# Nine more slabs of an encoder kernel's input projection as seven products of quarters, on one core

## What is computed

```
xa (1024)  ya (1024)  u, v (1024 each)  z (1024)  xbc (2048)  dt (16)  gates gA, gB, gC (1024 each)
branch A: xa -> conv over 4 tokens -> two small products (lg) -> linear recurrence, times gelu(ya)
branch B: gelu(u) * (layernorm(gelu(v)) mixed within blocks of 128 tokens)
branch C: silu(conv(xbc)) -> x, B, C of a chunked state-space scan; times silu(z); normalised
x += W_out(sum of sigmoid(gate) * projection of each branch)
x += cross attention over 256 memory tokens;  x += top-2 of 32 experts (width 512);  out = rmsnorm(x)
```

## Time and profile before

| what | value |
|---|---|
| median of 3 runs | 996.18 us |
| lowest and highest run | 995.7 and 999.54 us |
| span of the profiled execution, first to last instruction | 992.8 us |
| PE busy | 848.5 us, 85% of the span |
| PEld busy | 641.3 us, 65% |
| DVE busy | 293.7 us, 30% |
| ACT busy | 192.6 us, 19% |
| POOL busy | 211.2 us, 21% |
| HBM read | 283.08 MB, 286 GB/s over the span |

### The profile page before, as it was taken

The page is one execution under the profiler, slowest core; times in us unless marked ns, Lnnn a source line. Parts: engine busy times, 40 slices in busy tenths (PEclk is TensorE's granted clock), DMA queues, the critical chain, the costliest instruction groups (busy, mean ns, idle before and its releaser), DMA issues.

```text
span 992.8 us, 17255 instructions
## 1 busy us (share of the span) xinstructions
PE 848.5 (85%) x7608; PEld 641.3 (65%) x7608; DVE 293.7 (30%) x785; ACT 192.6 (19%) x354; POOL 211.2 (21%) x120
## 2 busy tenths in 40 slices
PE   8999999999999999999999999666676666666575
PEld 8888866888999999999479555333333333333342
DVE  2344101646164433342111552121221221121212
ACT  2321126851022000101111221111101111101102
POOL 1000000003999878994001000000000000000000
PEclk9999999999999999999999999987987998988987
DMA  9734524342454444444994799999999999999995
GB/s 304 217 126 158 196 101 170 128 170 85 170 212 171 171 169 166 157 161 167 430 363 158 314 426 426 426 428 427 426 428 425 428 427 428 426 426 426 426 427 203
DMA packets 62399, 285.24 MB, mean 287 GB/s; under 512 B 6692, under 2 KB 11640, under 8 KB 50168
## 3 DMA queue, kind: packets, MB, share of 16 engines
q1 hardware_dynamic: 52736, 278.96, 70.2%
q10 hardware_dynamic: 9592, 5.19, 2.0%
HBM read 283.08 MB, written 1.06 MB: 286 GB/s over the span
## 4 chain that ended last, share of the span: by engine, by line
PE 62%; DMA 28%; SPq 4%; another core or an unknown queue 2%; DVE 1%; POOL 1%; issue 1%; ACT 0%; DVEq 0%; POOLq 0%
PE bank L1639 20%; PE bank L1468 20%; DMA ring<-in_w_gate_up_dram 15%; DMA ring<-in_w_down_dram 10%; PE bank L1480 6%; PE bank L1822 5%; SPq L398 4%; DMA blk<-in_w_gate_up_dram 3%; PE bank L1844 2%; PE bank L1541 1%; PE bank L1791 1%; PE bank L1715 1%; PE bank L1695 1%; PE bank L1600 0%
## 5 line engine op out<-in xcount | busy, mean ns | idle before, releaser
L1468 PE MATMUL bank<-blk,ring 128*128 128x256 f32 x896 | 198.5, 383 | 0.8 <-DVE blk L1237 0.8
L1468 PEld LDWEIGHTS bank<-blk,ring 128*128 128x128 f32 x896 | 170.3, 191 | 25.5 <-issue 1.4
L1639 PE MATMUL bank<-ring 128*128 128x128 f32 x1088 | 127.4, 275 | 0.4 <-POOL ring L507 0.4
L1639 PEld LDWEIGHTS bank<-ring 128*128 128x128 f32 x1088 | 124.3, 192 | 0.7 <-issue 0.6
L1822 PE MATMUL bank<-ring,cbm 128*32 128x256 f32 x1088 | 80.5, 446 | 48.5 <-DMA ring<-in_w_gate_up_dram 48.1
L1639 PE MATMUL bank<-blk,ring 128*128 128x128 f32 x816 | 96.7, 275 | 0.1
L1639 PEld LDWEIGHTS bank<-blk,ring 128*128 128x128 f32 x816 | 94.1, 192 | 0.9 <-issue 0.8
L1822 PEld LDWEIGHTS bank<-ring,cbm 128*32 128x32 f32 x1088 | 40.1, 125 | 81.3 <-issue 61.7
L480 POOL TENSOR_TENSOR ring<-ring 128x1024 f32<-128x1024 f32 x17 | 40.1, 2356 | 241.9 <-PE bank L1601 230.9
L1326 DVE TENSOR_TENSOR cbm<-bank,gq 128x256 f32<-128x256 f32 x32 | 13.6, 424 | 251.3 <-PE bank L1791 251.3
L1822 PE MATMUL bank<-blk,cbm 128*32 128x256 f32 x768 | 57.9, 452 | 31.9 <-DMA blk<-in_w_gate_up_dram 31.9
(11 more groups left out here) (307 smaller groups left out, 842.5 us busy)
## 6 DMA issues: line engine op xcount, KB each, us to landing
ring<-in_w_gate_up_dram SPq DMA_DIRECT2D x34, 2048.0 KB, 49.9
blk<-in_w_gate_up_dram SPq DMA_DIRECT2D x24, 2048.0 KB, 50.3
ring<-in_w_in_dram SPq DMA_DIRECT2D x19, 2048.0 KB, 7.7
ring<-in_w_down_dram SPq DMA_DIRECT2D x18, 2048.0 KB, 49.5
blk<-in_w_down_dram SPq DMA_DIRECT2D x10, 2048.0 KB, 49.5
params<-in_w_gate_up_dram SPq DMA_DIRECT2D x6, 2048.0 KB, 50.0
ring<-in_w_kv_dram SPq DMA_DIRECT2D x4, 2048.0 KB, 7.9
params<-in_w_down_dram SPq DMA_DIRECT2D x3, 2048.0 KB, 51.2
```

Source lines behind the costliest of these rows:

```text
L1468: last = mm(ps[:, f * T:(f + 1) * T], w[:, k, c:c + P], src[:, k, :], start=k == 0, stop=k == KD - 1)
L1639: last = mm(ps[:, f * P:(f + 1) * P], wt[:, k, f * P:(f + 1) * P], xt[:, k, :], start=k == 0, stop=k == 3)
```

## The change

- Nine slabs go from the dense to the seven-product form: xbc 1 to 3, xa 0 and 1, z 0 and 1, v 0 and 1. Slab 0 of xbc, u, ya and the first slab of gA stay dense. There are 26 seven-product slabs instead of 17.
- Input sums of hT for them are made once, into a new place TE (block 6); the weight sums and the copied and added middles of slabs ahead of pA 0 live in blocks 5 and 8 (`weight_sums`, `middles`).
- Quarters are kept interleaved in a bank (`part`), so that two neighbouring quarters form one run of 256 tokens for each column tile. This holds for all 26 slabs.
- For xbc and xa DVE adds the products inside the banks (`conv_sums`), and conv_init and the taps read them there. z and v are folded into their tiles, and ACT then applies silu and gelu in place to halves of 1024 elements (`silu_z`, `gelu_v`). For v the tokens stand in the array and 256 columns of weights stream (`in_rows`).
- The eight lg units come four behind each v slab instead of two behind each v unit. DVE's exponents(0) and (1) move ahead of the fold of v, and its product on L983 behind it. The softplus part of ACT moves from the third conv_init to behind the small loads, and silu of two units is done behind each slab's `mids`.
- The banks of a seven-product slab are taken one at a time as its products come to them, not all four ahead of the first.
- PE waits for `read["xn"]` ahead of the q slabs.

The core of the diff (the new helpers, and where they are used):

```diff
+    for h in range(1, 4):
+        order += seven("xbc", h)
+    order += seven("xa", 0) + seven("xa", 1) + ["cs0"]
+    order += seven("z", 0) + [f"xs{i}" for i in range(4)] + seven("z", 1) + [f"cb{i}" for i in range(GROUPS)]
+    for h in range(2):
+        order += seven("v", h) + [f"lg{j}" for j in range(4 * h, 4 * h + 4)]
...
+        TA, TB, TE = (block(b).rearrange("p (q k t) -> p q k t", q=4, t=P) for b in (10, 9, 6))
+        EARLY = SEVEN["pA", 0]
+        def weight_sums(j):
+            two, one = (5, 8) if j < EARLY else (11, 14)
...
+        def part(ps, i):
+            return ps.rearrange("p (f j t) -> p j f t", f=2, j=2)[:, i]
...
@@ gpsimd
+            combos(hT, TE, first=(read["rx"], KD))
+            for name, h in (("xbc", 1), ("xbc", 2), ("xbc", 3), ("xa", 0), ("xa", 1), ("z", 0), ("z", 1), ("v", 0),
+                            ("v", 1)):
+                weights_1(name, h)
+                weights_2(name, h)
...
@@ scalar
+            def mids(name, h):
+                j = SEVEN[name, h]
+                if j == EARLY:
+                    act.wait_ge(sem["yA_ready"], 1)
+                if j:
+                    act.wait_ge(read["s"], 4 * j)
+                act.wait_ge(sem["product"], 6 * j + 2)
+                a.copy(middles(j)[0], part(bank(f"s{4 * j}"), 0)).then_inc(sem["mid_copied"], 1)
...
+                if i >= 2 and i % 2 == 0:
+                    mids("xbc", i // 2)
+                    silu_xbc(i - 2)
+                    silu_xbc(i - 1)
+                conv_init("xbc", i, lambda f: col("ccw", 3 * XBC_TILES + f), lambda f: col("ccb", f), 2 * i, xbcT)
...
+            for h in range(2):
+                mids("v", h)
+                for j in range(4 * h, 4 * h + 4):
                     ps = take(f"lg{j}")
                     a.activation(gxT[:, j, :], ps[:, 0:T], ACT.Sigmoid, bias=col("gxb", j))
                     a.activation(aT[:, j, :], ps[:, T:2 * T], ACT.Sigmoid, bias=col("gab", j)).then_inc(read["lg"], 1)
+                gelu_v(h)
...
@@ vector
+            def conv_sums(name, h):
+                j = SEVEN[name, h]
+                mid_a, _, mid_p, mid_q = middles(j)
+                b1, b2, b3 = (bank(f"s{4 * j + r}") for r in range(1, 4))
+                link(sums(j, part(b1, 1)))
+                dve.wait_ge(sem["product"], 6 * j + 6)
+                v.tensor_tensor(part(b2, 0), mid_a, part(b2, 0), ALU.add)
+                v.tensor_tensor(part(b2, 1), mid_p, part(b2, 1), ALU.add).then_inc(sem["pair_ready"], 1)
+                take(f"s{4 * j + 3}")
+                v.tensor_tensor(part(b1, 0), mid_q, part(b3, 0), ALU.add).then_inc(sem["pair_ready"], 1)
...
             for i in range(NX):
-                taps(f"xbc{i}", "ccw", XBC_TILES, 2 * i, xbcT)
+                if i >= 2 and i % 2 == 0:
+                    conv_sums("xbc", i // 2)
+                taps("xbc", i, "ccw", XBC_TILES, 2 * i, xbcT)
...
             dve.wait_ge(read["cs"], 1)
-            dve.wait_ge(read["cb"], GROUPS)
             exponents(0)
             exponents(1)
+            for h in range(2):
+                fold("v", h, rows_of(vN, h))
+            dve.wait_ge(read["lg"], KD)
+            link(v.tensor_tensor(gxT, gxT, xaT, ALU.mult))
...
@@ tensor
+            def strassen(name, h, x, t_, made, in_rows=False):
+                def product(i, wt, xt):
+                    if i % 2 == 0:
+                        banks_.append(begin(f"s{4 * j + i // 2}"))
+                    out_ = part(banks_[-1], i % 2)
+                    if in_rows:
+                        for k in range(4):
+                            last = mm(out_, xt[:, k, :], wt[:, k, :].rearrange("p (f t) -> p f t", f=2),
+                                      start=k == 0, stop=k == 3)
+                        return last
...
+            for h in range(1, 4):
+                strassen("xbc", h, hT, TE, 0)
+            for h in range(2):
+                strassen("xa", h, hT, TE, 0)
...
-            for i in range(2):
-                dense(f"z{i}", hT)
+            strassen("z", 0, hT, TE, 0)
...
-            for i in range(2, 4):
-                dense(f"z{i}", hT)
+            strassen("z", 1, hT, TE, 0)
...
-            pe.wait_ge(read["xa"], 4)
-            for i in range(4):
-                dense_rows(f"v{i}", hT)
-                for j in (2 * i, 2 * i + 1):
+            pe.wait_ge(read["s"], 4 * SEVEN["xa", 1] + 4)
+            for h in range(2):
+                strassen("v", h, hT, TE, 0, in_rows=True)
+                for j in range(4 * h, 4 * h + 4):
```

More of the change, by code:

```diff
@@ L921, in _, with sums @@
             last.then_inc(sem["d_ready"], 1)
-            convs = [0]
-            def taps(unit, w, tiles_, f0, acc):
+            def sums(j, out22):
+                mid_a, mid_u, mid_p, mid_q = middles(j)
+                b0, b1 = bank(f"s{4 * j}"), bank(f"s{4 * j + 1}")
+                dve.wait_ge(sem["mid_copied"], j + 1)
+                dve.wait_ge(sem["product"], 6 * j + 4)
+                link(v.tensor_tensor(mid_u, mid_a, part(b1, 1), ALU.add))
+                v.tensor_tensor(mid_q, mid_u, part(b1, 0), ALU.add)
+                v.tensor_tensor(mid_p, mid_u, part(b0, 1), ALU.add).then_inc(read["s"], 1)
+                dve.wait_ge(read["s"], 4 * j + 1)
+                return v.tensor_tensor(out22, mid_p, part(b1, 0), ALU.add)
@@ new lines, in fold @@
+            def fold(name, h, quarter):
+                j = SEVEN[name, h]
+                mid_a, _, mid_p, mid_q = middles(j)
+                b2, b3 = bank(f"s{4 * j + 2}"), bank(f"s{4 * j + 3}")
+                sums(j, quarter(1, 1)).then_inc(read["s"], 1)
+                dve.wait_ge(sem["product"], 6 * j + 6)
+                v.tensor_tensor(quarter(0, 0), mid_a, part(b2, 0), ALU.add)
+                v.tensor_tensor(quarter(0, 1), mid_p, part(b2, 1), ALU.add).then_inc(read["s"], 1)
+                take(f"s{4 * j + 3}")
+                v.tensor_tensor(quarter(1, 0), mid_q, part(b3, 0), ALU.add).then_inc(read["s"], 1)
@@ L927, in taps @@
+            def taps(name, i, w, tiles_, f0, acc):
                 convs[0] += 1
                 dve.wait_ge(sem["conv_init"], convs[0])
-                ps = bank(unit)
+                ps = bank(pair_unit(name, i))
                 for j in range(1, CONV):
@@ L1093, in in_two, with in_banks @@
-            def in_two(ps):
-                return ps.rearrange("p (f t) -> p f t", f=2)
-            def fold(name, h, out, f0):
-                j = SEVEN[name, h]
-                sums(j, quarter_of(out, f0, 1, 1)).then_inc(read["s"], 1)
+            def in_banks(j):
+                mid_a, _, mid_p, mid_q = middles(j)
+                b1, b2, b3 = (bank(f"s{4 * j + r}") for r in range(1, 4))
+                link(sums(j, part(b1, 0)))
+                yield part(b1, 0)
                 dve.wait_ge(sem["product"], 6 * j + 6)
-                v.tensor_tensor(quarter_of(out, f0, 0, 0), mid_a, in_two(part_of(j, 2, 0)), ALU.add)
-                v.tensor_tensor(quarter_of(out, f0, 0, 1), mid_p, in_two(part_of(j, 2, 1)), ALU.add).then_inc(read["s"], 1)
+                v.tensor_tensor(part(b2, 0), mid_a, part(b2, 0), ALU.add)
+                link(v.tensor_tensor(part(b2, 1), mid_p, part(b2, 1), ALU.add))
+                yield halves(b2)
@@ L1103, in fold @@
                 take(f"s{4 * j + 3}")
-                v.tensor_tensor(quarter_of(out, f0, 1, 0), mid_q, in_two(part_of(j, 3, 0)), ALU.add).then_inc(read["s"], 1)
+                link(v.tensor_tensor(part(b3, 0), mid_q, part(b3, 0), ALU.add))
+                yield part(b3, 0)
             def upper(tile, f0):
-                return tile[:, f0:f0 + 2, :].rearrange("p f (j t) -> p j f t", j=2)
-            def both(j):
-                return part_of(j, 2, 0, 2).rearrange("p (j f t) -> p j f t", j=2, f=2)
@@ L1112, in in_banks @@
[L1112 to L1122 removed]
+                return tile[:, f0:f0 + 2, :]
@@ L1545, in _ @@
             to_par(1)
-            for i in range(1, 8):
-                if i > 1:
-                    dense(f"xbc{i}", hT)
-                if i == 1:
-                    pe.wait_ge(sem["small_loaded"], 16 * SOON)
-                    ps = begin("dt0")
-                    for t in range(NT):
-                        for k in range(KD):
-                            last = mm(ps[:, t * HEADS:(t + 1) * HEADS], hT[:, k, t * P:(t + 1) * P], wdt[:, k, :],
-                                      start=k == 0, stop=k == KD - 1)
-                    end(last)
```

285 lines of the change are left out of this document (139 added, 146 removed).

## The result

| what | before | after |
|---|---|---|
| median, same chip, 4 runs each | 995.94 us | 984.05 us |
| lowest and highest | 995.64 and 999.54 | 982.98 and 985.31 |
| span of the profiled execution | 992.8 us | 982.8 us |
| PE busy | 848.5 us | 838.9 us |
| POOL busy | 211.2 us | 300.7 us |

The ratio is 0.987, 95% interval 0.985 to 0.989: faster by 11.9 us. The forecast was 983.5, range 981 to 989. The answers come from PE's front half; what stands behind it moved with it.

A forecast was written before the change was run, and what follows sets the result against it. PE bounds the first 500 us, the expert weights' loading the last 460. Savings of 9.6 (slabs) + 3.2 (v) - 0.1 (y0) = 12.7 us from 996.2 give 983.5 us, range 981 to 989.

The forecast's parts named there:

- Regimes: First 500 us are PE's own time, last 460 the expert weights'; what PE saves in front comes out whole at the end.
- Cost of the seven-product form: On PE: seven xbc, xa and z slabs at 12.50 instead of 13.87 us save 9.6 us; v 0 and 1 save 3.2.
- y0: Attention behind u0: table load and gelu on ACT delay w_ready, so y0 waits 0.1 us; bounds 0 and 1.5.
- Rival 3: Products don't get cheaper: interleaved banks slow streams of 128 or 256 columns, nine slabs take what they took; 996 us, chance 0.06.
- POOL at the start: POOL's sums for the first slab keep step, S4 done by 32.4; costs nothing, bounded at 1 us of stall.
- The chain on DVE: Copy, sums, adds, conv_init and taps per conv slab take about 9.6 us, shorter than PE's 12.50; costs nothing.
- rival 2: DVE's taps are held up by POOL's sums, 19.0 us per conv slab; 15.8 us slower, 1012 us, chance 0.05.
- the cover of 4 us: First conv chain ends at 54.8 and PE waits for its later banks only at 58.8, growing by 2.9 a slab.
- Rival 1: Small DVE instructions stand behind POOL's sums: eight router-weight scalings, 18.9 us, 8.8 covered; 984 to 993, say 988; chance 0.14.
- The low clock: Up to 99.54 PE holds 1.5 us beyond its five slabs, at mean clock 0.98; left in place as dt products stay.
- From span to time: Span 992.8 becomes 980.1; the median's 3.4 us above the span is kept, giving 983.5 us.
- the bounds: Bounds of v (2.4 to 3.4), y0 (0 to 1.5) and start (0 to 1) put the saving at 9.5 to 12.9 us.

The follow-up runs named there:

- the split: Narrow dt products cut in two halves, the second behind wider products: on the changed kernel 981.41 us (ratio 0.9856), on the kernel before 994.45 us (0.998).
- the seven-fold kernel: Changed kernel with 48 more scalings of the router weights ahead of the eight, 56 in all: 998.28 us, ratio 1.0018.
- four neutral relatives: Changed kernel with one edit each: router-weight scalings moved (983.98 us), sixteen more scalings (984.07), last gelu later (983.05), all four banks taken first (984.61).

## Why the prediction was right, point by point

**Regimes: right.** What was saved in the front arrived at the end: with the clock out of the comparison 12.7 us by the mark, and 11.8 to 13.0 by the time.

**Cost of the seven-product form: right.** The conv slabs take 12.50 us. They were not put back by themselves; the two profiles with the split give 6.5 us for the five of them, where 6.85 was forecast. The v slabs take 12.08, which is the 112 x 0.216 = 24.2 us for two that was taken from the dense stream's row, so a stream of 256 columns costs the same when its output is cut into two runs of 128. Taking the form away again costs 2.6 in the front for z (forecast 2.7) and 3.1 for v with y0 (forecast 3.1). Rival 3 is out.

**POOL at the start: right, with room.** The input sums, each of half as many elements as a sum of weights, take 1.26 us and not the 2.36 that I used as a bound, and S4 is the last of eight sums. POOL of the changed kernel in time:

```profile
13.74 1.26 POOL L523 TENSOR_TENSOR blk<-blk 128x512 f32<-128x512 f32 x1 [9.76 <-DVE blk L966]
...
18.99 2.34 POOL L495 TENSOR_TENSOR blk<-ring 128x1024 f32<-128x1024 f32 x1 [0.19 <-DMA ring<-in_w_in_dram]
...
26.15 2.36 POOL L512 TENSOR_TENSOR blk<-ring,blk 128x1024 f32<-128x1024 f32 x1
```

S4 is done at 28.5, not 32.4, before PE has begun the slab.

**The chain on DVE: right.** First and last steps of the first one:

```profile
46.79 0.42 DVE L982 TENSOR_TENSOR blk<-blk,bank 128x256 f32<-128x256 f32 x1 [15.80 <-ACT blk L660]
...
50.34 5.28 DVE L1032 SCALAR_TENSOR_TENSOR ring<-bank,first,ring 128x255 f32<-128x255 f32 x12 [0.76 <-ACT ring L669]
55.54 0.19 DVE L1059 TENSOR_TENSOR dtw<-dtw 128x32 f32<-128x32 f32 x1
55.76 2.45 DVE L1063 SCALAR_TENSOR_TENSOR dtw<-dtw 128x16 f32<-128x16 f32 x2
```

The copy came at 46.4 instead of 45.2 and the chain ended at 55.6 instead of 54.8; the cover of 4 us took that. The taps take 5.28 us for twelve beside POOL's sums, and as much without: in the seven-fold kernel one set runs from 103.53, while POOL is idle, in 5.28 us as well. So rival 2 is out. The last line shows the other kind: one of two products of 16 elements with both operands in SBUF takes 2.35 us, and the POOL sum it stood behind ran from 55.82 to 58.17. The Trainium skill (SBUF — State Buffer, section Who interferes with whom) says that the engine which comes second on the shared ports is blocked for the whole of the other's instruction, not slowed. The traces of the changed kernel agree: DVE's instructions of that kind take 2.39 us at most, beside sums of 2.35 to 2.40 us on POOL.

**Rival 1 had the right mechanism and the wrong size.** It priced one sum for each of the eight scalings, 18.9 us. They took 7.03: three were held. The price is per sum of POOL that falls into the time, and only the seven-fold kernel brings it beyond the cover.

**y0: right.** 0.2 us, forecast 0.1.

**The low clock: the step that failed.** "The dt products ahead of them stay, so I leave those 1.5 us in place." The low clock behind them cost 3.3 us in the changed profile and 1.7 in the one before, 1.6 more. That is most of what is missing at u0: of 12.8 - 10.75 = 2.05 us, 1.6 are the clock, 0.1 is the later start of the dt products (25.24 instead of 25.11) and 0.3 is the conv slabs' smaller gain. The instructions stayed, in this profile their cost did not. Kernels with the same products up to there show either cost, so it is not to be put down to the change. The times don't show it either. The split took about 2 us off both kernels (996.17 to 994.45, and 983.66 to 981.41). And the changed kernel and its four neutral relatives have ratios of 0.9861 to 0.9875, which is 12.5 to 13.9 us of 996.6; the 11.9 between the medians of the result lies within the scatter of four runs each. So what failed is the reading of one profile against another, not the forecast of the time.

**From span to time: two things in one term.** I kept 3.4 us between the span and the median. Profiled executions whose time is known take some 1.8 us more than their spans (984.55 for 982.8). By that the profiled one of before, at 992.8, took 994.6, so the 3.4 us held another 1.6 by which it was quicker than the median of its kernel. Keeping them came to taking 12.7 off the median, 996.2, and that is right as long as the low clock costs both kernels the same in most executions, which the times above bear out and no run shows directly. By the spans alone the forecast is off by 2.7 us: 980.1 was forecast and 982.8 measured. 1.8 of that arose up to the mark, 1.6 of it the clock, and 0.9 behind the mark, 0.7 of it in the expert stretch.

**How much of it is luck.** The medians scatter by more than the 0.6 us by which the number came out, two errors of 0.4 us in the sum cancelled, and the bounds had a slip: 9.6 + 3.4 is 13.0, not 12.9. That the sum holds to a few tenths rests on the marks of the two profiles with the split, one execution each.

## What to carry to other kernels

Where an engine is full and everything behind it waits on events, an instruction-by-instruction sum from rows of the same kernel can hold to a few tenths of a microsecond (12.4 against 12.8 at u0 here). Check the rest, the clock and the way from span to time, with the same care, since here they were worth 1.6 us each, more than a slab's gain. Before a loss in one profile is explained, look whether a second profile has it, and whether the times have it. A run of narrow streams on PE is worth splitting between wide ones where the clock falls behind it (3.2 us at the mark here). When asking what an instruction loses behind another engine's, count the other engine's instructions and its pauses, not one's own; and when PE is made to wait, look at the clock behind the wait (4.0 us on top of 10.6 here).

## What the runs showed of the hardware that was not expected

- Within or just behind 32 float32 products of 16 columns in a row (3.6 us at the higher clock), with PE busy throughout, the clock fell to its lower level in eleven profiles out of eleven that have them. In two runs of 1.8 us, with 1.8 us of wider streams between, it stayed at 1.00 in all three.
- The low stretch had two lengths for the same instructions, 3.4 and 6.8 us, costing 1.6 and 3.3 us. In the seven profiles with the longer one the clock had fallen 2.6 to 3.2 us behind the start of these products, in the four with the shorter one 3.4 to 4.5 us behind it.
- A DVE instruction that takes 0.16 us in a row of its kind can take 2.39 us beside POOL sums of 2.35 to 2.40 us, and the loss in a row of them does not grow with their number as long as POOL pauses: 8 of them were through at 83.7, and 24 at 84.5 in a profile that lies 1.6 us earlier, both in the pause behind the same four sums.
- PE can stand 2.6 to 2.9 us ahead of the instructions behind its last branch without a wait that the profile shows, in two of fourteen profiles. It stays open why.
